# One decoder block on one core: output statistics of two heads on two column halves, own blocks of all heads in one group

## The reference

```
scores[t, s] = sum_d q[t, d] * k[s, d] * exp(b[t, d] - b[s, d])     for s <= t
o[t]         = sum_s scores[t, s] * v[s]
o            = rms_norm(o, out_gain) * silu(g)                       over the 128 channels of a head
```

## Time and profile before

| | |
|---|---|
| median of 3 runs | 793.69 us |
| profiled execution | 794.33 us |
| its span | 792.6 us |
| granted TensorE clock | 0.999 of full |
| PE busy | 784.2 us, 99% |
| POOL busy | 489.7 us, 62% |
| DVE busy | 410.4 us, 52% |
| ACT busy | 216.2 us, 27% |

### The profile page before, as it was taken

One profiled execution on the slowest core, in us unless ns is written; L12 is line 12 of the kernel. 1 busy time (PEld: TensorE's weight loads), 2 busy tenths in 40 slices (PEclk: granted clock), 3 DMA queues, 4 the chain that ended last, 5 costly groups with the idle time before them and its releaser, 6 DMA issues.

```text
span 792.6 us, 12362 instructions
## 1 busy us (share of the span) xinstructions
PE 784.2 (99%) x4604; PEld 639.1 (81%) x4604; DVE 410.4 (52%) x580; ACT 216.2 (27%) x436; POOL 489.7 (62%) x325
## 2 busy tenths in 40 slices
PE   8999999999999999999999999999999999999998
PEld 6788878888777787778888888888888888888886
DVE  4795488946566565725467666660000567640000
ACT  6200754356422555733122222210000122210000
POOL 4666645677455756656666666766666667666563
PEclk9999999999999999999999999999999999999999
DMA  8244221233522011034223232232232322323320
GB/s 282 81 143 171 87 82 62 75 133 107 186 73 87 28 39 44 2 106 160 88 98 106 81 106 82 103 106 85 101 105 80 107 90 96 106 91 121 132 79 26
DMA packets 23548, 77.99 MB, mean 98 GB/s; under 512 B 2723, under 2 KB 3499, under 8 KB 23380
## 3 DMA queue, kind: packets, MB, share of 16 engines
q1 hardware_dynamic: 19964, 69.00, 25.9%
q10 hardware_dynamic: 3544, 8.44, 3.0%
HBM read 75.31 MB, written 4.21 MB: 100 GB/s over the span
## 4 chain that ended last, share of the span: by engine, by line
PE 94%; DVE 3%; DMA 1%; POOL 1%; issue 0%; SPq 0%; ACT 0%; DVEq 0%; POOLq 0%
PE bank L413 26%; PE bank L415 26%; PE bank L414 26%; PE bank L752 2%; PE bank L797 2%; PE bank L785 2%; PE bank L507 1%; PE bank L508 1%; PE bank L509 1%; DMA x<-in_xT 1%; PE bank L556 1%; POOL wsp L333 1%; PE bank L437 1%; PE bank L668 1%; DVE pc L1522 1%; DVE tot L1328 0%
## 5 line engine op out<-in xcount | busy, mean ns | idle before, releaser
L333 POOL TENSOR_TENSOR wsp<-wraw,wsp 128x1024 fp32r<-128x1024 f32 x124 | 305.8, 2466 | 10.4
L331 POOL TENSOR_SCALAR wsp<-wraw 128x1024 fp32r<-128x1024 f32 x124 | 135.9, 1096 | 237.4 <-PE bank L415 153.0
L413 PE MATMUL bank<-hhi,wsp 128*128 128x512 f32 x352 | 141.4, 402 | 1.8 <-DVE hlo L1239 1.2
L415 PE MATMUL bank<-hhi,wsp 128*128 128x512 f32 x352 | 137.3, 390 | 0.0
L414 PE MATMUL bank<-hlo,wsp 128*128 128x512 f32 x352 | 137.2, 390 | 0.0
L413 PE MATMUL bank<-ghi,wsp 128*128 128x512 f32 x256 | 100.4, 392 | 0.0
L415 PE MATMUL bank<-ghi,wsp 128*128 128x512 f32 x256 | 99.7, 390 | 0.0
L413 PE MATMUL bank<-uhi,wsp 128*128 128x512 f32 x256 | 99.7, 389 | 0.0
L414 PE MATMUL bank<-glo,wsp 128*128 128x512 f32 x256 | 99.6, 389 | 0.0
L414 PE MATMUL bank<-ulo,wsp 128*128 128x512 f32 x256 | 99.6, 389 | 0.0
L415 PE MATMUL bank<-uhi,wsp 128*128 128x512 f32 x256 | 99.6, 389 | 0.0
(11 more groups left out here) (271 smaller groups left out, 1052.9 us busy)
## 6 DMA issues: line engine op xcount, KB each, us to landing
wraw<-in_w SPq DMA_DIRECT2D x126, 512.0 KB, 3.3
bias_skewed<-bias_lines ACTq DMA_DIRECT2D x1, 2048.0 KB
bias<-bias_skewed ACTq DMA_DIRECT2D x1, 2048.0 KB, 8.9
x<-in_xT ACTq DMA_DIRECT2D x1, 2048.0 KB, 9.4
out<-x ACTq DMA_DIRECT2D x8, 256.0 KB, 2.0
x<-in_xT SPq DMA_DIRECT2D x3, 512.0 KB, 7.5
x<-in_xT SPq DMA_DIRECT2D x2, 256.0 KB, 5.0
wraw<-in_w SPq DMA_DIRECT2D x4, 128.0 KB, 8.4
```

The lines of the kernel that those rows point to most:

```text
L331: pool.tensor_scalar(whi[:, two, :], wraw[:, raw, :], 1.0, 0.0, ALU.mult, ALU.add).then_inc(w_hi, 1)
L333: pool.tensor_tensor(wlo[:, two, :], wraw[:, raw, :], whi[:, two, :].bitcast(F32), ALU.subtract).then_inc(w_split, 1)
L413: pe.matmul(out_, wh, mh, start=first, stop=False)
L415: return pe.matmul(out_, wl, mh, start=False, stop=last)
```

## The change

The own blocks of all four heads go into one group between the projection `ks` and the first level. They fill all 512 columns of bank 7, so `own` claims one bank instead of two, and the counter of banks starts at 1. `keep_own` waits for all of them and copies both halves in a row. Bank 6 is released at the start by a plain increment behind the clearing of `near`.

The sums of squares are taken for two heads together. `output_stats(pair)` issues two matmuls with 64 columns of ones each: head 2·pair writes partitions 0 to 63 of bank 6 and head 2·pair + 1 writes 64 to 127. The groups stand behind `ga0` and `ga2`; behind `ga1` there is none and behind `ga3` the `cst` matmuls come directly. On ACT one Ln over both goes to the tile `tmp`, and four Exps of 64 partitions write each head's 1/rms to both halves of the partitions of `rstd`. The squares of heads 2 and 3, the key copies and the copies to `oahi` follow in a new order.

```diff
-        OWN_BANK = {"st_ks": 2, "st_kw": 3, "st_q0": 4, "st_q1": 5, "st_o0": 6, "st_o1": 6, "st_o2": 6, "st_o3": 6}
+        OWN_BANK = {"st_ks": 2, "st_kw": 3, "st_q0": 4, "st_q1": 5}
...
-            sc_banks = [0]
+            sc_banks = [1]
...
-            def own(pair):
-
-                to = None
-                for h in (2 * pair, 2 * pair + 1):
+            def own():
+
+                to = sc_bank()
+                for h in range(HG):
                     pe.wait_ge(kq_ready, h + 1)
-                    to = sc_bank() if to is None else to
                     for t in range(ST):
-                        c = h % 2 * P + 32 * t
+                        c = h * P + 32 * t
...
             project("kc")
-            own(0)
             project("vc")
-            own(1)
             project("ks")
+            own()
             near_level(0)
...
-            def output_stat(h):
+            def output_stats(pair):
                 pe.wait_ge(part_lo, PART["kw"] + 1)
-                pe.wait_ge(pair_read, 4 + h)
-                stat(f"st_o{h}", ones[:], sq[:, h % 2, :], to=bank[6])
+                pe.wait_ge(pair_read, 4 + pair)
+                pe.wait_ge(stat_in, stats[0] + 2)
+                stats[0] += 2
+                for n in range(2):
+                    pe.matmul(bank[6][64 * n:64 * n + 64, :], ones[:, 0:64], sq[:, n, :], start=True, stop=True,
+                              skip_group_check=True).then_inc(stat_out, 1)
...
-            output_stat(0)
+            output_stats(0)
...
-            for h in range(1, HG):
-                project(f"ga{h}")
-                output_stat(h)
-
+            project("ga1")
+            project("ga2")
+            output_stats(1)
+            project("ga3")
...
-                act.wait_ge(stat_out, 7 if h < 2 else 7 + h)
+                act.wait_ge(stat_out, 7 if h < 2 else 10)
...
+            def inverse_rms_of_two():
+                outs[0] += 2
+                act.wait_ge(stat_out, outs[0])
+                link(act.activation(tmp[:], bank[6][:], ACT.Ln, scale=1.0 / P, bias=eps))
+                act.sem_inc(pair_read, 1)
+                act.wait_ge(rs_used, rs[0])
+                for n in range(2):
+                    rows = slice(64 * n, 64 * n + 64)
+                    act.activation(rstd[0:64, n, :], tmp[rows, :], ACT.Exp, scale=-0.5)
+                    act.activation(rstd[64:128, n, :], tmp[rows, :], ACT.Exp, scale=-0.5).then_inc(rs_ready, 1)
+                rs[0] += 2
...
-            def keep_own(pair):
-                dve.wait_ge(sc_done, 4 * pair + 4)
-                dve.copy_predicated(flat[:, 256 * pair:256 * pair + 256], mask[:, 5 * 256:],
-                                    bank[6 + pair][:, 0:256]).then_inc(sc_kept[pair], 1)
+            def keep_own():
+                dve.wait_ge(sc_done, 8)
+                for pair in range(2):
+                    c = slice(256 * pair, 256 * pair + 256)
+                    last = dve.copy_predicated(flat[:, c], mask[:, 5 * 256:], bank[7][:, c])
+                last.then_inc(sc_kept[1], 1)
...
             raw("kc", kc_raw[:], blocks_in)
-            keep_own(0)
             low(0)
             raw("vc", vc_raw[:], blocks_in)
-            keep_own(1)
             low(1)
             raw("ks", ksn[:], raw_copied)
+            keep_own()
             for n in range(7):
                 dve.wait_ge(sc_done, SC_LEVEL[n])
                 advance(n)
```

More of the change, by code:

```diff
@@ L1107, in _, with out_of_head @@
             gelu_exp(1)
[L1108 to L1116, removed]
+            def inverse_rms_of_two():
[9 more added lines that the diff above has]
+                rs[0] += 2
+            def out_of_head(h):
                 act.wait_ge(oa_f, h + 1)
                 act.activation(oahi[:, h, :], o_ring[:, h % 2, :], ACT.Copy).then_inc(oa_hi, 1)
-                if h == 0:
-                    act.wait_ge(skew_out, 16)
-                    act.dma_start(bias[:], skewed.rearrange("h p u -> p h u")).then_inc(bias_in, 16)
+            inverse_rms_of_two()
+            square_o(2)
+            square_o(3)
+            key_low_again("ks")
+            key_low_again("kw")
+            out_of_head(0)
+            act.wait_ge(skew_out, 16)
+            act.dma_start(bias[:], skewed.rearrange("h p u -> p h u")).then_inc(bias_in, 16)
+            out_of_head(1)
+            inverse_rms_of_two()
+            out_of_head(2)
+            act.wait_ge(cst_done, 1)
+            for g in range(2):
+                act.activation(pcT[g][:], cst_bank[g][:], ACT.Copy).then_inc(cst_kept, 1)
+            out_of_head(3)
             for qb in range(ST):
@@ L1380, in _ @@
             link(dve.memset(near[:], 0.0))
+            dve.sem_inc(sc_kept[0], 1)
             dve.wait_ge(line_out, 32)
```

## The result

The changed kernel takes 795.35 us in the median of 12 runs (793.98 to 796.28), against 793.62 before. The ratio is 1.002, with an interval of 1.0013 to 1.0027: slower, by 1.7 us, where 1.9 us faster was forecast from the same median. The profiled execution took 795.71 us, its span 793.9.

The account below looks back on a forecast made before the run. TensorE (PE), busy 784.2 of 792.6 us, was taken as the bound. Gains of 1.0 (statistics), 0.7 (own blocks) and 0.3 (wait) sum to 2.0 us, from the median 793.69 to 791.7; range 790.9 to 792.9.

Parts of the forecast that it names:

- The statistics: Output sums of squares on PE: four matmuls of 0.86 us become two groups of 1.22, a gain of 1.0 us.
- the halves side by side: Each statistics group's two 64-column halves run concurrently on PE; the rival, one after the other, 793.4 us, had chance 0.06.
- The entry and the exit: Changing the array's division around a statistics group on PE adds 0.09 us in front and 0.11 behind.
- The own blocks' saving: One own group directly before the first level instead of separate groups on PE: gain 0.7 us, worked out as 0.78 or 0.64.
- the prediction's lower bound: For the own blocks' merge on PE, counting only two entries, two exits and two tails: a gain of 0.64 us.
- The wait and keep_own: PE's 0.30 us wait before the second level goes, gain 0.3; keep_own's copies on DVE cost nothing to 0.2 us.
- The unknown: keep_own's copies on DVE were taken as not held by POOL's L333; if held, a cost of 0.1 to 0.2 us.
- F + 256a: Own blocks and first level as one PE group, fixed cost plus cost per record: 2.39 us instead of 3.17.
- The rival of the clock: Behind the new group of 2.4 us of 32-column matmuls the clock falls to 1.2 GHz: 797.2 us, chance 0.04.

Follow-up runs that it names:

- e3_own_behind_vc: The changed kernel with the group of all own blocks behind vc, one projection before the first level: 792.19 us, ratio 0.9982.
- e5_two_and_two: The kernel before with the new statistics, own blocks of heads 0 and 1 behind vc, 2 and 3 behind ks: 791.88 us, ratio 0.9978.
- e6: e5_two_and_two with 32 small matmuls of 32x32 on ones added in front of kc: 793.89 us, ratio 1.0005.
- e1: The kernel before with only the own blocks moved in front of the first level, the four statistics unchanged: 796.27 us, ratio 1.003.
- e8: The changed kernel with the load of the weights for nq3 made to wait until the first level is done: 794.68 us, ratio 1.0012.
- e7: e5_two_and_two with 16 small matmuls of 32x32 on ones added in front of kc: 792.75 us, ratio 0.9988.

## Why the prediction was wrong

**The statistics were right**, term by term: 1.20 for a group where 1.22 was forecast, 1.12 us gained where the sum had 1.0, the halves side by side. The entry and the exit are there: 212.88 to 213.20 is 0.32, 214.21 to 214.54 is 0.33.

**The own blocks' saving was right in kind.** e3_own_behind_vc saves 0.24 and e5_two_and_two 0.62 with the wait, so some 0.3 for each group less, and two groups less would give about the 0.64 of the prediction's lower bound. No run shows both savings without a stop; in the changed kernel 0.3 of the 0.7 is measured beside the stop.

**The wait and keep_own.** The wait of 0.30 went, also in e5_two_and_two, where it is not mixed with a stop. The unknown, whether a predicated copy is held under POOL's L333, is settled: it isn't. Both copies take 0.77 us, L333 ran all the while, and they end before it does.

```profile
94.93 2.37 POOL L333 TENSOR_TENSOR wsp<-wraw,wsp 128x1024 fp32r<-128x1024 f32 x1
95.08 0.77 DVE L1327 COPY_PREDICATED near<-mask,bank 128x256 f32<-128x256 uint8 x2 [0.72 <-PE bank L539]
98.94 1.23 DVE L1349 TENSOR_TENSOR tot<-f 128x1024 f32<-128x1024 f32 x1 [3.09 <-PE bank L555]
```

L1349 also confirms how were read. The stop had carried it past the end of L333 at 97.30, and it took 1.23 us, not 3.46.

**The step that failed** is "Afterwards all 256 stand in one group, ... F + 256a". The 256 there are matmul records; with the weight loads it is 512, two whole blocks. The step prices a longer group by the cost of a record in a short one, as if the supply of instructions had no rate of its own. None of the groups of small matmuls before is longer than 272 records (L447 and a level), and none of them stops: the packet due in the group of the earlier trace rows started at 111.08, before PE's 1729th instruction at 111.56. So no row there shows what a stop costs, but the instruction queue stood on its page, with 28 packets, and I never read it. In the changed kernel a block was used up in 1.3 us (94.14 to 95.41), and the next one was in use at 98.11, 4.0 us behind that crossing at 94.14. In e6 that took 3.1 us (95.90 to 98.99), in e1 3.4 and in e8 3.7. The difference, up to 2.7 us, was the missing term.

**The rival of the clock** named the right place, with 0.04, but not what happened. It was to be a run of 2.4 us of 32-column matmuls. The changed kernel never had one: its run was cut after 2 us by the stop, and the fall came behind that. In the traces with a fall the stop before it is 1.97, 2.28 and 2.51 us long, and no trace with a shorter stop or none has a fall there. (One of 25 runs of the kernel before, without a trace, also took 796.10 at 0.997.) e5_two_and_two, with some 1.9 us of such matmuls in a row, keeps 1.0; a longer run without a stop wasn't tried, so the rival's own rule is not refuted. The price was sized at one projection's 5.5 us and came to 1.55. With the stop at 2.51 it makes 4.06, and less the 1.1 and 0.6 gained it leaves some 2.4 us in a run with the fall and 0.8 in one without. Measured are 2.0 and 0.5 (medians 795.61 and 794.14 against 793.62), so the sum over one trace is 0.3 to 0.4 too high, and the rest is open; the median of all is 1.7.

The best version is e5_two_and_two, 791.88 us, 1.6 less than before and 3.5 less than the changed kernel. It has the new statistics, puts only half of the own blocks in front of the first level, and lies within the forecast range, though it is not the kernel that was forecast. It is safe only while its instructions lie where they lie: 32 small matmuls more in front of it cost 2.0 us, where the same 32 cost the kernel before 0.9.

## What to carry to other kernels

A bound engine can run out of instructions. Before merging groups of small matmuls, count their instructions, weight loads and both passes included. A whole block of 256 inside such work is the danger: here it was used up in 1.3 us, and the next one was in use only after 3.1 to 4.0. Then a saving of tenths turns into a stop of microseconds and, behind it in most runs, a slower clock. The count alone doesn't decide. e5_two_and_two has 404 matmuls and loads within 4 us and no stop, because there a block ends 7 instructions into the group and not 135, as in the changed kernel and in e6, and the packet had started 3.5 us before the group:

```profile
94.67:98.67 4.00, 4.00 (x202) 3.62 (x202) 3.10 (x3) 3.96 (x8) 3.46 (x2) 1.00 0.04 13
```

"Issue" in the list of waits, in the middle of a run of equal instructions, is the sign; the count of instructions up to it, compared over two kernels whose positions differ, is the proof. And whether a dense group stops depends on every instruction in front of it, so an edit far ahead can move a stop into it.

## What was unexpected of the hardware

The blocks' period of 256 is exact over 768 instructions, from the 1217th to the 1985th, and through code of several kinds. From the crossing to the use of the next block it takes 3.1 to 4.0 us at four of the stops and 6.0 at that of e7, where weights moved. The packet itself is 0.93 to 1.33 of that, and 1.3 lie between its end and PE's first matmul at all five. In the profiled execution of the changed kernel the granted clock went to 0.50 some 1.4 us behind PE's return from an idle stretch of 2.5 us, and stayed there for 3.4 us; in a third of the runs of the same kernel it did not fall.
